# First block's attention with weights applied before the transposes and values computed feature-major

## The chip, the cores and the metric

The kernel runs on one core of one Trainium2 chip. The metric is the device time of one execution in microseconds (us), as the median of the runs shown. Engines are called by the profile's names: PE (matmuls, with PEld for the load of a stationary operand), DVE, ACT, POOL and SP.

## The reference, cut to what matters

Two transformer blocks run one after the other on 512 tokens of width 1024, all in float32. Only the attention of the first block is touched. For each of 8 heads (64 wide) and each block of 128 queries it computes three softmax attentions, and adds them with three gates per head and token:

```python
p_c = masked_softmax(s_c, cmp_end[None, :] <= t[:, None])   # compressed keys, 31 of them
o_c = einsum("bgrqk,bkgd->bqgrd", p_c, v_cmp)
p_s = masked_softmax(s_s, ...);  o_s = einsum(...)          # selected keys
p_w = masked_softmax(s_w, ...);  o_w = einsum(...)          # window
o = gb[..., 0:1] * o_c + gb[..., 1:2] * o_s + gb[..., 2:3] * o_w
...
mixed = concatenate([rmsnorm(y_conv, norm_conv_out), rmsnorm(y_att, norm_attn_out)], axis=-1)
h = h + rmsnorm(mixed @ w_out, norm_mix_post)
```

With 8 blocks of 64 keys and 16 selections every causal key is selected, so the selected and the window branch see the same causal keys and differ in their projections only.

## The kernel before, in words

Activations lie feature-major (128 features x 512 tokens) and weights stream in units of 128x2048, each split into a high and a low part, so that one product of 128x128 weights with 512 tokens is three matmuls (`products`, lines 417 to 419). Engines run side by side and meet at semaphores; each engine's own instructions run in the order written.

The attention is a software pipeline over turns `t` from -4 to 33, written out once for each engine (PE line 1016, ACT line 1238, DVE line 1484). Turns -4 to -1 hold the compressed branch, one block of 128 queries each (`c_scores`, `c_turn`, `c_values`, `c_combine`). Turns 0 to 31 start one job each. Job `j` is query block `j // 8`, head pair `j % 8 // 2` and branch `j % 2` (selected or window); its number of keys is 128, 256, 384 or 512 by block. A job goes through these steps:

- PE `scores(t)` (line 965): both heads' scores and the mask, into banks `2*(j%2)` and the next.
- DVE `maxima(t)` (line 1434): row maxima and their negatives. ACT `exps(t)` (line 1202): exponentials with row sums.
- PE `turn(t-1)` (line 981): transposes the probabilities, 2 x (1 to 4) pieces of 128x128, into bank 4 (and 5 from job 16 on). It waits for its exponentials, and for ACT to have copied the transposes of the job before out of bank 4.
- ACT `copy_turned(t-1)` (line 1213) and, from job 16, DVE `copy_turned` (line 1443): PSUM to SBUF.
- PE `values(t-2)` (line 995): probabilities stationary, 64 value columns moving, so the result lies tokens-major.
- DVE `combine(t-2)` (line 1450): reciprocal of the sum, times the gate, then for each head a multiply-add of 128x64 into `o_all`.

In a turn PE does scores, then chunks of input projections as filler (3 chunks of 3 matmuls in turns -4 to 7, 2 in turns 8 to 19, none later), then the turn, then the values. ACT does the exponentials of `t` before the copy of the older job. DVE also carries the short convolution and its norm in turns 8 to 30, and the weight splits. The convolution's column sums are on PE in turn 23, after POOL has added squares (line 2577); POOL then computes an inverse root in 12 small steps (`inverse_root`, line 701), which PE spreads to rows in turn 26 (line 1041).

After the loop PE fills with `mixed_products` (first half of the output projection). The attention norm takes row sums of squares from ACT, a root, a reciprocal, four scalings by DVE, and 16 transposes by PE (`mixed_turn`, line 1045) that turn `o_all` feature-major. Then a loop over `k` from 4 to 7 (line 1066) does the second half.

The second block's attention (`layer_pe`, line 2000) already computes its values with the value columns stationary and the two heads in the two column halves of the array (line 2133), and scales its probabilities on POOL (line 2597).

Of the kernel before, what the change touches and what calls it, by code (L numbers as in the profile page):

```python
# [31 lines left out]
P = 128  # L32
T = 512
# [68 lines left out]
def build(nc, w, x, mem, pos, pack, tables, cmask, w2, wg, rope2, out):  # L102
    ctx = ExitStack()
    with ctx:
# [55 lines left out]
        e_c = place("e_c", [P, 2, 2 * P], F32, b)  # L160
        pt_c = place("pt_c", [P, 2, 2 * P], F32, b)
        kvc = place("kvc", [P, 2, T], F32, a)
        vtok = place("vtok", [P, QB, 2 * P], F32, a)
        cosT = place("cosT", [P, T], F32, a)
# [6 lines left out]
        perm = place("perm", [P, P], F32, a)  # L171
        wg_s = place("wg_s", [P, 8 * 24], F32, a)
# [14 lines left out]
        probT = place("probT", [P, 2, 2, T], F32, b)  # L187

# [506 lines left out]
        ao_sq, ao_std, ao_inv, ao_n, ao_t = (sem("attn_norm_" + n) for n in ("squares", "std", "inv", "scaled", "turned"))  # L695
# [19 lines left out]
        LAG_TURN, LAG_VALUES, LAG_BACK = 1, 2, 3  # L715

# [15 lines left out]
        CONV_SQ_AT = {11: (0,), 16: (1,), 19: (2,), 22: (3,)}  # L732
        AT_CONV_SUM, AT_CONV_INV, AT_CONV_ROWS = 23, 24, 27
# [41 lines left out]
        def wide(j):  # L775
            return j >= 16

# [24 lines left out]
        def mixer1_pe(pe):  # L802
# [141 lines left out]
            def c_turn(i):  # L944
                pe.wait_ge(j_exp, i + 1)
                if i >= 1:
                    pe.wait_ge(j_pta, i)
                for e in range(2):
                    c0 = (2 * (i % 2) + e) * P
                    mm = pe.transpose(bank[:, 4, c0:c0 + P], e_c[:, i % 2, e * P:(e + 1) * P], ident[:, :])  # L950
                mm.then_inc(j_t, 1)

            def c_values(i):
                pe.wait_ge(j_pta, i + 1)
                if i == 0:
                    pe.wait_ge(vblk_ready, 4)
                else:
                    pe.wait_ge(j_o, i)
                for e in range(2):
                    mm = pe.matmul(bank[:, 6, e * 4 * HD:(e + 1) * 4 * HD], pt_c[:, i % 2, e * P:(e + 1) * P],  # L960
                                   vblk[:, :], start=True, stop=True)
                mm.then_inc(j_pv, 1)
# [18 lines left out]
            def turn(j):  # L981
                i = j // 8
                pe.wait_ge(j_exp, QB + 2 * (j + 1))
# [5 lines left out]
                for e in range(2):  # L989
                    for k in range(i + 1):  # L990
                        b_, c0 = (4 + e, k * P) if wide(j) else (4, (2 * e + k) * P)
                        mm = pe.transpose(bank[:, b_, c0:c0 + P], prob[:, j % 2, e, k * P:(k + 1) * P], ident[:, :])  # L992
                mm.then_inc(j_t, 1)

            def values(j):
                i, m, br, g = job(j)
                pe.wait_ge(j_pta, QB + j + 1)
                if wide(j):
                    pe.wait_ge(j_ptd, turned_by_dve(j))
                pe.wait_ge(j_o, QB + 2 * j)  # L1000
                for e in range(2):
                    c0 = (j % 2) * 2 * HD + e * HD
                    for k in range(i + 1):
                        mm = pe.matmul(bank[:, 6, c0:c0 + HD], probT[:, j % 2, e, k * P:(k + 1) * P],  # L1004
                                       vtok[:, k, br * P + g * HD:br * P + (g + 1) * HD], start=(k == 0), stop=(k == i))
                mm.then_inc(j_pv, 1)
# [9 lines left out]
            for t in range(-QB, JOBS + LAG_VALUES):  # L1016
                if t < 0:
                    c_scores(t + QB)
                elif t < JOBS:
                    scores(t)  # L1020
                gated_chunks(GATED_AT.get(t, 0))
                if t == -QB:
                    compressed_values()
                if t == JOBS:
                    pe.wait_ge(mix_lo, 4)
                    pe.wait_ge(lo_ready, U_OUT + 1)
                if t >= JOBS:
                    mixed_products(0, (t - JOBS,), range(4))
                if -QB <= t - LAG_TURN < 0:
                    c_turn(t - LAG_TURN + QB)  # L1030
                elif 0 <= t - LAG_TURN < JOBS:
                    turn(t - LAG_TURN)
                if -QB <= t - LAG_VALUES < 0:
                    c_values(t - LAG_VALUES + QB)
                elif t - LAG_VALUES >= 0:
                    values(t - LAG_VALUES)
# [8 lines left out]
            def mixed_turn(m):  # L1045
                if m == 0:
                    pe.wait_ge(ao_n, QB)
                if m >= 2:
                    pe.wait_ge(mix_lo, 4 + m - 1)
                for b_ in range(QB):  # L1050
                    mm = pe.transpose(bank[:, 6 + m % 2, b_ * P:(b_ + 1) * P], o_all[:, b_, m * P:(m + 1) * P], ident[:, :])
                mm.then_inc(ao_t, 1)

            pe.wait_ge(j_exp, QB + 2 * JOBS)
            pe.wait_ge(lo_ready, U_OUT + 2)
            mixed_products(1, (0, 1), range(4))
# [21 lines left out]
        def mixer1_act(act):  # L1078
# [112 lines left out]
            def c_e(i):  # L1191
                act.wait_ge(c_sub, i + 1)
                act.activation(e_c[:, i % 2, :], e_c[:, i % 2, :], ACT.Exp).then_inc(j_exp, 1)

            def c_copy(i):
                act.wait_ge(j_t, i + 1)
                if i >= 2:
                    act.wait_ge(j_pv, i - 1)
                c0 = 2 * (i % 2) * P
                act.activation(pt_c[:, i % 2, :], bank[:, 4, c0:c0 + 2 * P], ACT.Copy).then_inc(j_pta, 1)  # L1200

            def exps(j):
                n = (j // 8 + 1) * P
                act.wait_ge(j_neg, QB + j + 1)
                if j >= 2:
                    act.wait_ge(j_t, QB + j - 1)
                if j >= 4:
                    act.wait_ge(j_rec, j - 3)
                for e in range(2):
                    act.activation(prob[:, j % 2, e, 0:n], bank[:, 2 * (j % 2) + e, 0:n], ACT.Exp,  # L1210
                                   bias=jsm(j, 2, e), accum_out=jsm(j, 4, e)).then_inc(j_exp, 1)

            def copy_turned(j):
                n = (j // 8 + 1) * P
                act.wait_ge(j_t, QB + j + 1)
                if j >= 2:
                    act.wait_ge(j_pv, QB + j - 1)
                if wide(j):
                    act.activation(probT[:, j % 2, 0, 0:n], bank[:, 4, 0:n], ACT.Copy).then_inc(j_pta, 1)
                else:  # L1220
                    act.activation(probT[:, j % 2, :, 0:n], bank[:, 4, :].rearrange("p (e c) -> p e c", e=2)[:, :, 0:n],
                                   ACT.Copy).then_inc(j_pta, 1)

            def squares_of_block(b_):

                act.wait_ge(j_o, QB + 2 * 8 * (b_ + 1))
                if b_ >= 2:
                    act.wait_ge(ao_sq, b_ - 1)
                act.activation(ctmp[:, b_ % 2, :], o_all[:, b_, :], ACT.Square, accum_out=small[:, 32 + b_:33 + b_]).then_inc(ao_sq, 1)
# [8 lines left out]
            for t in range(-QB, JOBS + LAG_TURN):  # L1238
# [6 lines left out]
                if -QB <= t - LAG_TURN < 0:  # L1245
                    c_copy(t - LAG_TURN + QB)
                elif t - LAG_TURN >= 0:
                    copy_turned(t - LAG_TURN)
# [19 lines left out]
            act.wait_ge(ao_sq, QB)  # L1268
            act.activation(small[:, 36:40], small[:, 32:36], ACT.Sqrt, bias=eps_c[:, 0:1], scale=1.0 / 512).then_inc(ao_std, 1)
            for k in range(MEM_EARLY):  # L1270
                memory_hi(k)
            for m in range(4):
                act.wait_ge(ao_t, m + 1)
                act.activation(x_hi[:, 4 + m, :], bank[:, 6 + m % 2, :], ACT.Copy, scale=col("attn_out", m)).then_inc(mix_hi, 1)
# [11 lines left out]
        def mixer1_dve(dve):  # L1286
# [114 lines left out]
            def c_softmax(i):  # L1401
# [3 lines left out]
                if i >= 2:  # L1405
# [1358 lines left out]
```

## Time and profile before

| | |
|---|---|
| median of 3 runs | 2245.42 us (2244.32 to 2248.05) |
| profiled execution, own time | 2247.24 us |
| its span, first to last instruction | 2245.0 us |
| mean granted TensorE clock | 0.997 of 2.4 GHz |
| busy: PE, PEld, DVE, ACT, POOL | 2220.2, 1815.0, 1280.5, 845.4, 248.0 us |
| PE share of the chain that ended last | 87% |

A timeline row is: start in us, length in us, engine, line, operation, tiles, shapes, count, and in brackets the idle time before it with what ended it. The length of a PE row includes the array's latency, so the time that a group takes is read from its start to the start of what follows. A float32 matmul shows as two records, each with its load. A windows row is: stretch, length, then busy us and instruction count for PE, PEld, DVE, ACT, POOL, then the granted clock, the DMA share and GB/s.

### The profile page before, as it was taken

The page shows a single profiled execution, that of the slowest core. Times are in us where ns is not written, and L with a number is a line of the kernel's source. Part 1 is how long each engine was busy: PE and PEld are TensorE (multiplying, and loading weights), DVE is VectorE, ACT ScalarE, POOL GpSimd, SP SyncE. Part 2 cuts the span into 40 slices and gives each one's busy share as a digit, 9 for nine tenths or more (in the row PEclk, how much of TensorE's full clock was granted, in tenths as well). Part 3 has the DMA queues.
Part 4 walks back from the last instruction along what each step waited for, and adds up shares of the span by engine and source line. Part 5 has one row for each costly group of instructions (what it writes and reads, how often), then busy time and mean ns, then how long its engine had stood idle before and what let it go on. Part 6 is the DMA issues. An engine that isn't in the chain of part 4 may idle for free.

```text
span 2245.0 us, 29099 instructions
## 1 busy us (share of the span) xinstructions
PE 2220.2 (99%) x11292; PEld 1815.0 (81%) x11292; DVE 1280.5 (57%) x1948; ACT 845.4 (38%) x1299; POOL 248.0 (11%) x273
## 2 busy tenths in 40 slices
PE   9999999999999999999999999999999999999999
PEld 7877888898888888886678888888887668888887
DVE  6467656445444225999874444333889884544422
ACT  5545454354333225233544333222322543433321
POOL 3000032011000001013231000001003232000000
PEclk9999999999999999999999999999999999999999
DMA  6221033112222231321122222223321112322222
GB/s 222 101 76 57 20 118 129 55 70 100 101 105 93 94 113 71 113 75 57 56 77 85 103 93 94 103 102 108 107 81 57 39 69 82 113 101 104 94 100 87
DMA packets 30484, 203.44 MB, mean 91 GB/s; under 512 B 3504, under 2 KB 4144, under 8 KB 6704
## 3 DMA queue, kind: packets, MB, share of 16 engines
q1 hardware_dynamic: 29088, 197.34, 24.7%
q10 hardware_dynamic: 1296, 4.72, 0.6%
q8 instruction: 68, 1.11, 0.2%
q14 instruction: 32, 0.26, 0.0%
HBM read 199.95 MB, written 2.10 MB: 90 GB/s over the span
## 4 chain that ended last, share of the span: by engine, by line
PE 87%; DVE 8%; issue 2%; POOL 1%; ACT 1%; DMA 0%; ACTq 0%; DVEq 0%; POOLq 0%
PE bank L417 25%; PE bank L419 25%; PE bank L418 25%; DVE cy L2333 3%; PE bank L2133 1%; PE bank L2112 1%; PE bank L1004 1%; PE bank L2120 1%; DVE w_lo L303 1%; PE bank L975 1%; POOL acc L326 1%; PE bank L2012 1%; PE bank L992 1%; PE bank L1595 1%; PE bank L1572 1%
## 5 line engine op out<-in xcount | busy, mean ns | idle before, releaser
L417 PE MATMUL bank<-x_hi,w_hi 128*128 128x512 f32 (+1 forms) x2032 | 790.3, 389 | 5.7 <-DVE x_lo L1768 2.3
L419 PE MATMUL bank<-x_hi,w_lo 128*128 128x512 f32 (+1 forms) x2032 | 775.0, 381 | 0.0
L418 PE MATMUL bank<-x_lo,w_hi 128*128 128x512 f32 (+1 forms) x2032 | 774.2, 381 | 0.0
L303 DVE TENSOR_TENSOR w_lo<-w_raw,w_hi 128x2048 fp32r<-128x2048 f32 x167 | 386.2, 2312 | 412.6 <-ACT w_hi L299 412.6
L299 ACT ACTIVATE w_hi<-w_raw 128x2048 fp32r<-128x2048 f32 x167 | 319.7, 1916 | 585.9 <-PE bank L419 584.0
L417 PEld LDWEIGHTS bank<-x_hi,w_hi 128*128 128x128 f32 x2032 | 382.3, 188 | 83.4 <-issue 6.5
L419 PEld LDWEIGHTS bank<-x_hi,w_lo 128*128 128x128 f32 x2032 | 382.1, 188 | 74.8
L418 PEld LDWEIGHTS bank<-x_lo,w_hi 128*128 128x128 f32 x2032 | 382.6, 188 | 72.5 <-issue 2.9
L417 PE MATMUL bank<-f_hi,w_hi 128*128 128x512 f32 (+1 forms) x572 | 213.3, 373 | 0.0
L418 PE MATMUL bank<-f_lo,w_hi 128*128 128x512 f32 (+1 forms) x572 | 213.2, 373 | 0.0
L419 PE MATMUL bank<-f_hi,w_lo 128*128 128x512 f32 (+1 forms) x572 | 213.2, 373 | 0.0
L2333 DVE SCALAR_TENSOR_TENSOR cy<-la,gains,cy 128x512 f32<-128x512 f32 x240 | 172.8, 788 | 0.0
L565 DVE TENSOR_TENSOR bank<-bank,rbc 128x512 f32<-128x512 f32 x66 | 46.0, 697 | 167.7 <-PE bank L419 159.7
L418 PEld LDWEIGHTS bank<-f_lo,w_hi 128*128 128x128 f32 x572 | 107.7, 188 | 18.9
L417 PEld LDWEIGHTS bank<-f_hi,w_hi 128*128 128x128 f32 x572 | 107.7, 188 | 18.9
L419 PEld LDWEIGHTS bank<-f_hi,w_lo 128*128 128x128 f32 x572 | 107.7, 188 | 18.8
L326 POOL TENSOR_TENSOR acc<-acc,sq 128x512 f32<-128x512 f32 (+1 forms) x48 | 77.6, 1617 | 144.2 <-ACT sq L310 140.5
L2259 ACT ACTIVATE lprob<-lprob,small 128x129 f32<-128x129 f32 x128 | 50.5, 396 | 102.9 <-DVE small L2413 102.9
L554 ACT ACTIVATE f_hi<-bank 128x512 f32 x66 | 39.5, 598 | 115.5 <-DVE bank L571 115.5
L573 DVE TENSOR_TENSOR f_lo<-bank,f_hi 128x512 f32 x66 | 45.7, 692 | 58.4 <-ACT f_hi L554 58.4
L326 POOL TENSOR_TENSOR acc<-sq 128x512 f32<-128x512 f32 (+1 forms) x8 | 14.4, 1802 | 444.3 <-ACT sq L310 444.3
L552 ACT ACTIVATE silu<-bank 128x512 f32<-128x512 f32 x66 | 38.8, 588 | 54.7 <-DVE bank L565 54.5
(356 smaller groups left out, 2627.4 us busy)
## 6 DMA issues: line engine op xcount, KB each, us to landing
w_raw<-w_d SPq DMA_DIRECT2D x184, 1024.0 KB, 4.8
out_d<-h SPq DMA_DIRECT2D x8, 256.0 KB, 6.4
h<-x_d ACTq DMA_DIRECT2D x3, 512.0 KB, 9.3
tab<-rope_d ACTq DMA_DIRECT2D x2, 768.0 KB, 4.3
memT<-mem_d ACTq DMA_DIRECT2D x1, 1024.0 KB, 4.9
w_raw<-w_d SPq DMA_DIRECT2D x2, 256.0 KB, 3.9
h<-x_d ACTq DMA_DIRECT2D x2, 256.0 KB, 5.7
w_raw<-w_d SPq DMA_DIRECT2D x1, 512.0 KB, 6.6
```

The source lines that it names most:

```text
L299: act.activation(w_hi[:, u.slot, :], w_raw[:, u.slot, :], ACT.Copy).then_inc(hi_ready, 1)
L303: dve.tensor_tensor(w_lo[:, u.slot, :], w_raw[:, u.slot, :], w_hi[:, u.slot, :], ALU.subtract).then_inc(lo_ready, 1)
L326: pool.tensor_tensor(acc[:, 0:width], sq[:, 0, 0:width] if k == 1 else acc[:, 0:width], sq[:, k % 2, 0:width], ALU.add).then_inc(acc_ready, 1)
L417: pe.matmul(dst, wh[:, k, cols], hi[:, kx_, at:at + width], start=start, stop=False)
L418: pe.matmul(dst, wh[:, k, cols], lo[:, kx_, at:at + width], start=False, stop=False)
L419: return pe.matmul(dst, wl[:, k, cols], hi[:, kx_, at:at + width], start=False, stop=stop)
L552: act.activation(silu[:, :], g, ACT.Silu).then_inc(silu_done, 1)
L554: act.activation(pick(f_hi, j, i), up, ACT.Copy).then_inc(f_hi_done, 1)
L565: dve.tensor_tensor(g, g, rbc[:, :], ALU.mult).then_inc(gu_scaled, 1)
L573: dve.tensor_tensor(pick(f_lo, j, i), up, pick(f_hi, j, i), ALU.subtract).then_inc(f_lo_done, 1)
L2259: act.activation(row, row, ACT.Exp, bias=asm(j, 0, e), scale=-1.0, accum_out=asm(j, 4, e)).then_inc(A["exp"], 1)
L2333: dve.scalar_tensor_tensor(out=cy[:, m, :], in0=src, scalar=wt, in1=cy[:, m, :], op0=ALU.mult, op1=ALU.add).then_inc(l_tap, 1)
```

## The change

1. The weight of a branch (gate over row sum) is multiplied into the probabilities by POOL before the transposes, one instruction per job (and per compressed block), the last operand broadcast. DVE's `combine` becomes `weights` (reciprocal and gate only), done one turn after the scores.
2. The transposes and the copies come three turns after the scores (`LAG_J = 3`) instead of one. Probabilities and their transposes get a third buffer. In a turn PE does scores, turn, filler chunks, values.
3. The values of the three branches of a head pair are one accumulation group: value columns stationary (64 wide), transposed probabilities moving (128 columns), head 0 into partitions 0 to 63 and head 1 into 64 to 127 of one bank. 16 such groups, at odd turns, replace 32 `values` and 4 `c_values`; one DVE copy of 128x128 puts each into `o_all`, now feature-major.
4. The attention norm squares on ACT, adds four tiles on DVE (`add_squares`), takes column sums on PE, and spreads the inverse root back over rows; DVE multiplies four tiles by it. The 16 transposes go.
5. On POOL the three convolution adds and the inverse root now stand between the scalings, at turns 17, 20, 23 and 25.

```diff
+        LAG_J, PAIRS = 3, QB * 4
+        CONV_ADD_AT = {17: 1, 20: 2, 23: 3}
+        def value_pair(t):
+            if t == JOBS + 2:
+                return PAIRS - 1
+            return (t - 5) // 2 if t % 2 and 5 <= t < JOBS + 2 else None
...
             def turn(j):
                 i = j // 8
-                pe.wait_ge(j_exp, QB + 2 * (j + 1))
+                pe.wait_ge(j_scaled, QB + j + 1)
                 pe.wait_ge(j_pta, QB + j)
...
+            def values(q):
+                i, m, _, g = job(2 * q)
+                pe.wait_ge(j_pta, QB + 2 * q + 2)
...
+                dst = [bank[HD * e:HD * e + HD, 6, 0:P] for e in range(2)]
                 for e in range(2):
+                    pe.matmul(dst[e], vblk[:, m * HD:(m + 1) * HD], pt_c[:, i, e * P:(e + 1) * P], start=True, stop=False)
+                for br in range(2):
                     for k in range(i + 1):
+                        v = vtok[:, k, br * P + g * HD:br * P + (g + 1) * HD]
+                        for e in range(2):
+                            mm = pe.matmul(dst[e], v, turned_of(2 * q + br)[:, e, k * P:(k + 1) * P],
+                                           start=False, stop=(br == 1 and k == i))
...
-            for t in range(-QB, JOBS + LAG_VALUES):
+            for t in range(-QB, JOBS + LAG_J):
...
+                if -QB <= t - LAG_J < 0:
+                    c_turn(t - LAG_J + QB)
+                elif t - LAG_J >= 0:
+                    turn(t - LAG_J)
                 gated_chunks(GATED_AT.get(t, 0))
...
+                    mixed_products((t - JOBS) // 2, ((t - JOBS) % 2,), range(4))
+                if value_pair(t) is not None:
+                    values(value_pair(t))
...
+            mixed_products(1, (1,), range(4))
             pe.wait_ge(lo_ready, U_OUT + 3)
+            pe.wait_ge(ao_sum, QB)
+            column_sums(pe, bank[:, 7, 0:QB], o_sq[:, :]).then_inc(ao_step, 1)
             mixed_products(2, (0,), range(4))
+            pe.wait_ge(ao_step, AO_INV)
+            pe.wait_ge(j_o, PAIRS)
+            spread(pe, bank[:, 6, :], small[:, 36:40]).then_inc(ao_step, 1)
             mixed_products(2, (1,), range(4))
...
# ACT
-                if -QB <= t - LAG_TURN < 0:
-                    c_copy(t - LAG_TURN + QB)
-                elif t - LAG_TURN >= 0:
-                    copy_turned(t - LAG_TURN)
+                if -QB <= t - LAG_J < 0:
+                    c_copy(t - LAG_J + QB)
+                elif t - LAG_J >= 0:
+                    copy_turned(t - LAG_J)
...
# DVE
+                if -QB <= t - 1 < 0:
+                    c_weights(t - 1 + QB)
+                elif 0 <= t - 1 < JOBS:
+                    weights(t - 1)
+                if 0 <= t - LAG_J < JOBS and wide(t - LAG_J):
+                    copy_turned(t - LAG_J)
+                if value_pair(t - 1) is not None:
+                    values_out(value_pair(t - 1))
+X
+            for t in range(-QB, JOBS + 1):
...
+                elif t - 1 >= 0:
+                    n = ((t - 1) // 8 + 1) * P
+                    p = prob_of(t - 1)[:, :, 0:n]
+                    pool.wait_ge(j_w, t)
+                    pool.tensor_tensor(p, p, jsm(t - 1, 8).unsqueeze(2).to_broadcast([P, 2, n]), ALU.mult).then_inc(j_scaled, 1)
+                if t in CONV_ADD_AT:
...
+                if t == AT_CONV_INV + 1:
+                    inverse_root(pool)
```

## Rows read from the trace of the kernel before

**Rows 1.** The page, busy time of each engine

```profile
PE 2220.2 (99%) x11292; PEld 1815.0 (81%) x11292; DVE 1280.5 (57%) x1948; ACT 845.4 (38%) x1299; POOL 248.0 (11%) x273
```

**Rows 2.** Windows, turns 24 to 31

```profile
220.00:252.00 32.00, 30.49 (x231) 23.53 (x229) 27.35 (x67) 19.18 (x49) 3.68 (x13) 1.00 0.16 61
```

**Rows 3.** Timeline of PE: first rows of turns 20, 24, 32, and of the last loop

```profile
207.90 0.59 PE L975 MATMUL bank<-kTx,qT 64*128 64x384 f32 x1
...
223.19 0.69 PE L975 MATMUL bank<-kT,qT 64*128 64x512 f32 x1
...
255.26 0.48 PE L417 MATMUL bank<-x_hi,w_hi 128*128 128x512 f32 x1
...
277.93 0.47 PE L417 MATMUL bank<-x_hi,w_hi 128*128 128x512 f32 x1
```

**Rows 4.** Timeline of PE, turn 29: turn, values, next scores

```profile
244.56 1.06 PE L992 MATMUL bank<-ident,prob 128*128 128x128 f32 x8
245.46 1.90 PE L1004 MATMUL bank<-vtok,probT 128*128 128x64 f32 x16
247.29 0.69 PE L975 MATMUL bank<-kTx,qT 64*128 64x512 f32 x1
```

**Rows 5.** The chain that ended last: one compressed block's values

```profile
129.60 0.87 PE bank L960 x4
```

**Rows 6.** Timeline of PE in the second block: values in column halves, their neighbours

```profile
1060.34 0.39 PE L418 MATMUL bank<-x_lo,w_hi 128*128 128x512 f32 x1
1060.57 0.40 PE L419 MATMUL bank<-x_hi,w_lo 128*128 128x512 f32 x1
1060.89 0.66 PE L2133 MATMUL bank<-lband,lv 128*64 128x128 f32 x8
...
1099.77 0.39 PE L2133 MATMUL bank<-lband,lv 128*64 128x128 f32 x4
1100.09 0.48 PE L2112 MATMUL bank<-lq 64*128 64x256 f32 x1
```

**Rows 7.** Timelines of DVE (turns 24, 25, 28) and ACT (copy of turn 28)

```profile
224.57 1.22 DVE L1439 TENSOR_REDUCE jcol<-bank 128x2 f32<-128x1024 f32 x1 [0.76 <-PE bank L978]
...
228.77 1.23 DVE L1439 TENSOR_REDUCE jcol<-bank 128x2 f32<-128x1024 f32 x1
...
241.07 1.22 DVE L1439 TENSOR_REDUCE jcol<-bank 128x2 f32<-128x1024 f32 x1
...
243.87 0.59 ACT L1219 ACTIVATE probT<-bank 128x512 f32<-128x512 f32 x1
```

**Rows 8.** Timelines of DVE and ACT, turn 21

```profile
212.84 0.95 DVE L1439 TENSOR_REDUCE jcol<-bank 128x2 f32<-128x768 f32 x1
...
215.16 0.49 ACT L1219 ACTIVATE probT<-bank 128x384 f32<-128x384 f32 x1
```

**Rows 9.** Lines by form, POOL: busy us, mean ns, then idle before

```profile
L326 POOL TENSOR_TENSOR acc<-acc,sq 128x512 f32<-128x512 f32 x42 | 73.2, 1743 | 135.4 <-ACT sq L310 132.3
L2597 POOL TENSOR_TENSOR lprob<-lprob,small 128x256 f32<-128x256 f32 x64 | 39.1, 612 | 155.4 <-DVE small L2401 155.4
...
L2569 POOL TENSOR_TENSOR acc<-rbc 128x512 f32<-128x512 f32 x1 | 1.0, 1040 | 6.2 <-ACT rbc L399 6.2
```

**Rows 10.** Timeline of POOL: first and last of the 12 root steps

```profile
228.94 0.20 POOL L706 TENSOR_TENSOR jcol<-jcol 128x4 f32<-128x4 f32 x1 [6.79 <-DVE jcol L1481]
...
232.05 0.20 POOL L713 TENSOR_TENSOR rcol_c<-jcol 128x4 f32<-128x4 f32 x1
```

**Rows 11.** Timeline of DVE, turn 30: low halves of the convolution

```profile
251.88 1.41 DVE L1514 SCALAR_TENSOR_TENSOR x_lo<-cv,gains,x_hi 128x512 fp32r<-128x512 f32 x2
```

**Rows 12.** Timeline of PE, second block: column sums behind a wait

```profile
1063.28 1.05 PE L335 MATMUL bank<-ones,la 128*128 128x1 f32 x8 [1.73 <-POOL la L2611]
```

**Rows 13.** Windows around those column sums

```profile
1062.00:1064.00 2.00, 0.72 (x7) 0.72 (x7) 1.92 (x9) 0.30 (x1) 1.97 (x3) 1.00 0.17 70
...
1066.00:1068.00 2.00, 2.00 (x12) 1.03 (x10) 1.92 (x8) 0.58 (x2) 0.74 (x2) 0.51 0.00 0
```

More of the change, by code:

```diff
@@ L159, in build @@
         b = [a[0]]
[L160 to L161 removed]
+        e_c = place("e_c", [P, QB, 2 * P], F32, b)
         kvc = place("kvc", [P, 2, T], F32, a)
         vtok = place("vtok", [P, QB, 2 * P], F32, a)
+        cos_at = a[0]
         cosT = place("cosT", [P, T], F32, a)
@@ L171, in build @@
         perm = place("perm", [P, P], F32, a)
+        b = [a[0]]
+        pt_c = place("pt_c", [P, QB, 2 * P], F32, b)
+        o_sq = place("o_sq", [P, T], F32, b)
         wg_s = place("wg_s", [P, 8 * 24], F32, a)
@@ L694, in build @@
             "turned_copied_dve", "pv", "out"))
-        ao_sq, ao_std, ao_inv, ao_n, ao_t = (sem("attn_norm_" + n) for n in ("squares", "std", "inv", "scaled", "turned"))
+        ao_sq, ao_sum, ao_step, ao_n = (sem("attn_norm_" + n) for n in ("squares", "added", "step", "scaled"))
+        AO_SUMS, AO_STD, AO_INV, AO_ROWS = 1, 2, 3, 4
+        j_scaled = sem("job_scaled")
         JOBS = QB * 8
@@ L949, in c_turn @@
                     c0 = (2 * (i % 2) + e) * P
-                    mm = pe.transpose(bank[:, 4, c0:c0 + P], e_c[:, i % 2, e * P:(e + 1) * P], ident[:, :])
+                    mm = pe.transpose(bank[:, 4, c0:c0 + P], e_c[:, i, e * P:(e + 1) * P], ident[:, :])
                 mm.then_inc(j_t, 1)
[L953 to L962, printed above, removed]
             def scores(j):
@@ L1235, in memory_hi @@
                 square(act, NORM_MEM, k, memT[:, k, :], MEM)
-            for t in range(-QB, JOBS + LAG_TURN):
+            for t in range(-QB, JOBS + LAG_J):
                 if t < 0:
@@ L1455, in combine, with values_out, add_squares @@
                 dve.tensor_tensor(jsm(j, 8), jsm(j, 6), gate[:, i, 6 * m + 1 + br:6 * m + 5 + br:3], ALU.mult).then_inc(j_w, 1)
[L1456 to L1466 removed]
+            def values_out(q):
+                i, m, _, g = job(2 * q)
+                dve.wait_ge(j_pv, q + 1)
+                dve.tensor_copy(o_all[:, m, i * P:(i + 1) * P], bank[:, 6, 0:P]).then_inc(j_o, 1)
+            def add_squares(b_):
+                dve.wait_ge(ao_sq, b_ + 1)
+                dve.tensor_reduce(o_sq[:, b_ * P:(b_ + 1) * P], ctmp[:, b_ % 2, :].rearrange("p (m t) -> p t m", m=4),
+                                  AX, ALU.add).then_inc(ao_sum, 1)
             def memory_lo(k):
@@ L1483, in mixer1_dve @@
             dve.wait_ge(gate_ready, QB)
-            for t in range(-QB, JOBS + LAG_VALUES):
+            for t in range(-QB, JOBS + LAG_J + 1):
                 if t < 0:
```

178 lines of the change are left out of this document (69 added, 109 removed).

## The prediction

> **What bounds the kernel now.** I read the page first: PE is busy 99% of the span and no other engine over 57% (DVE) [rows 1], so only what lengthens or shortens PE's own sequence counts. Then the windows of the attention: in turns 24 to 31 PE still shows 30.5 of 32.0 us, but DVE has 27.4 [rows 2], so relief for PE is soon met by DVE or by waits. Then PE's timeline, for the time of each stage. Turns 20 to 23 take 15.3 us, turns 24 to 31 take 32.1, and from there to the last loop over k it is 22.7 [rows 3]. Last, the timelines of DVE and ACT beside PE, for the chain that a turn hangs on. All sums are against the profiled execution (2247.24 us, span 2245.0); the median of the runs is 2245.42, and I put the same difference on it.
>
> **Prices on PE.** Old values: 16 records from 245.46 to 247.29, 0.115 us each [rows 4]. A transpose is 0.11 (8 in 0.90) [rows 4], a compressed block's values 0.87 [rows 5]. The new form stands in the trace already: the second block's values are also 128 rows by 64 columns with 128 moving columns, heads in column halves. There 8 records take 0.66, of which the last 0.27 is latency, so 0.056 each; the group starts 0.32 after its neighbour where neighbours are 0.23 apart, and 4 records take 0.32 to the next scores [rows 6]. So a group costs 0.056 per record and about 0.1 at each end. A head pair has 12, 20, 28 or 36 records in query blocks 0 to 3: 0.87, 1.32, 1.77, 2.2 us, against 0.92, 1.84, 2.76, 3.66 for the two old jobs. The end pieces are where a rule speaks against the change. The Trainium skill (TensorEngine Tiling (Array Packing), Tiling Modes, Key Properties) says that a change of tiling mode drains the array. The rows agree that there is a price, 0.1 at each end; if a full latency of 0.27 went at both ends of 16 groups, the sum would be some 5 us worse.
>
> **Before turn 20.** PE has filler chunks there and sets the pace. Removed: 4 compressed blocks at 0.87 = 3.5; values of jobs 0 to 17, 8x4 + 8x8 + 2x12 = 120 records = 13.8; transposes of jobs 17 and 18, now later, 12 x 0.11 = 1.3. Added: pairs 0 to 7, 4 x 0.87 + 4 x 1.32 = 8.8. Net 9.8 less. Against it: a turn now stands ahead of the chunks that used to cover its wait, and it still waits for ACT's copy of the job before, which is queued behind the newest exponentials. I take 0.4 for several short waits net of one that goes (between 0 and 2). **9.4 gained.**
>
> **Turns 20 to 31, the step that I think decides.** Without chunks, PE's turn(t-3) waits for copy(t-4), which ACT issues in turn t-1 behind exps(t-1). The longer lag does not loosen this: the chain still runs from the newest scores. For 512 keys: first score to the reduction 1.38 (223.19 to 224.57), reduction to ACT's copy 2.80 (241.07 to 243.87), copy to the turn 0.69 [rows 3, 4, 7], turn to values 0.90 [rows 4], together 5.77. At odd t the values of a whole pair follow, 2.2, and only then the next scores: at least 8.0 us for two jobs. Before, the same chain with one job's 1.83 was 7.6 for two, hidden by PE's own work of some 3.9 per job (a turn is 4.0 [rows 3], of it 0.90 and 1.83 [rows 4], the rest scores, about 1.2). So block 3 is as slow as before although PE works only 2 x 1.2 + 2 x 0.9 + 2.2 = 6.4 us in those 8. For 384 keys: 1.15 (the 1.38 less the shorter scores) + 2.32 + 0.49 + 0.10 [rows 8] + 0.66 + 1.77 = 6.5.
>
> Two new waits lie on top, both of PE for POOL. The scaling: 0.612 for 256 elements, and 1.04 for 512 where one operand is read twice; 1.74 where two are [rows 9]. I take 2.1 for 1024 and 1.6 for 768, as its second operand is a column; the ends are 0.6 (no growth with size) and 3.5.
> - Turn 23: the column sums of the convolution wait for POOL's third add, now behind scaled(22), which waits for DVE's weights of turn 23. From the scores of turn 22: 1.15; DVE's turn 22 2.8 (reduction 0.95 [rows 8], and by estimate 0.5 for small ones, 0.5 and 0.2 for copies, 0.65 for the squares); reduction and weights of turn 23 1.5; scaling 1.6; add 1.3 (1.04 to 1.74 [rows 9]); sums 1.0 [rows 12]: 9.4. With 6.5 for turns 20 and 21: 15.9 against 15.3, **0.6 lost**.
> - Turn 26: PE's spread waits for the inverse root, now behind scaled(24). From the scores of turn 24: 1.38; DVE's turn 24 4.0 (4.20 before [rows 7] less 0.4 for two multiply-adds plus 0.2 for the copy); reduction and weights of turn 25 1.7; scaling 2.1; root 3.3 [rows 10]; spread 0.5: turn 27 starts at 13.0. Scores 1.2, turn 0.9 and a pair of 1.77 bring turn 28 to 16.9, and two rounds of 8.0 turn 32 to 32.9, against 32.1: **0.8 lost**.
>
> **After turn 31.** PE has 1.8 more (two transposed jobs later), 4.4 for two pairs instead of 3.66 for two jobs (0.75), 1.5 for column sums and spread instead of 16 transposes at 0.11 (0.3 less), and some 0.3 for restarts. DVE's turn 30 carries two low halves (1.41 [rows 11]), add_squares (about 0.65, half of a 1024-element reduction [rows 7]) and a copy, so exps(31) and the turn behind it come some 1.4 late. The norm's chain (copy, squares, add; then root and reciprocal) is covered by blocks of 12 products, 12 x 0.23 = 2.7 [rows 6]; the first scaled tile, behind three memory tiles on DVE, is not quite: 0.5. **4.5 lost.** What POOL, ACT and DVE do of the memory norm keeps its place behind this. No transfer moves; SP's queue and the four DMAs of ACT are untouched.
>
> **The clock.** In the second block a wait of 1.73 for POOL followed by one-column sums [rows 12] was followed by a granted clock of 0.51, the lower of its two levels (1.2 GHz), after 1.00 [rows 13]. The change makes two such places, turn 23 (a wait of 1.6, then sums) and turn 26 (3 us idle). At the lower level the next scores (1.2) take twice as long, and behind the spread some 0.6 more: 1.0 or 1.9. I take one of the two, 1.4 (ends 0 and 2.9). The Trainium skill (TensorE: Matmul & The Clock Gate, Part 1) says that the slow level is the default and activity lifts it; the rows agree.
>
> **Sum:** -9.4 + 0.6 + 0.8 + 4.5 + 1.4 = -2.1: 2245.4 - 2.1 = **2243.3**.
>
> **Rivals.**
> - *PE's work decides everywhere.* Removed in all: 3.5 + 320 records x 0.115 = 36.8 + 1.8; added 384 records x 0.056 = 21.5, 16 x 0.2 = 3.2, sums and spread 1.5: 15.9 less, 2229.5. For it: 99% busy. Against it: turn 29 of the trace starts 0.69 after the start of the 0.59 us copy, not when PE is free [rows 4, 7]. 0.10.
> - *The clock holds.* Without the 1.4: 2241.9. For it: the pauses have other lengths than the one seen. 0.22.
> - *POOL is dear.* 3.5 for 1024 elements and 2.6 for 768, as in the dearest row: 1.4 later at turn 26, 1.0 at turn 23: 2245.7. For it: DVE's convolution and POOL read the same memory at once. Against it: 0.612 in the second block, beside a busy DVE. 0.11.
> - *Slower: the low clock stays.* From turn 24 on PE works 6.4 of 8.0 us a pair; at 0.51 [rows 13] it needs 12.5, 4.5 more than the chain, and small matmuls follow that may not lift the clock. From 1.5 pairs on (-2.1 + 6.7) the kernel is past no change by more than can be told; for two pairs it is -2.1 + 9.0: 2252.3. Against it: before, all of turns 24 to 31 ran at 1.00 [rows 2]. 0.12.
> - *My forecast*, 0.45, with 2239 to 2247.5 as its own range (the ends of the waits and of the clock above).
>
> **How the numbers follow.** A measurement of this kernel can tell about 0.2%, 4.5 us, from no change: 2240.9 and 2249.9. Faster: the first rival whole, four tenths of the second, a sixth of the forecast: 0.26. Slower: most of the last rival and a little of the forecast: 0.14. The rest, 0.60, is within. Range: 2236.5 to 2250.0, which leaves out the first rival and most of the slower one.
>
> **What would show it.** Right: PE rows of the 128x64 form at 0.056; turn 20 about 9 us earlier than before; pairs of turns from 28 on 8.0 us apart, with PE idle before the transposes, released by ACT's copy; a wait for POOL before the column sums of turn 23 and before the spread of turn 26; the last loop at most 4 us earlier. Wrong: transposes that start as soon as PE is free; turns 24 to 31 in under 29 us (PE's work decides) or over 36 (the clock); scalings over 3 us.

## The result, and the profile after

The changed kernel takes 2250.38 us (median of ten runs), the kernel before 2245.59 us in the same series: the ratio is 1.0018, 95% interval 1.001 to 1.0026, which is 2.2 to 5.8 us. By the medians it is 4.8 us slower where 2.1 us faster was forecast, and 0.4 us above the range. One of the ten runs of the kernel before took 7339 us; without it their median is 2245.42 us. The profiled execution took 2251.5 us with a span of 2249.7 us (2247.24 and 2245.0 before).

The page of the changed kernel, busy time of each engine, shows what was meant to happen: against [rows 1] PE works 9 us less, and POOL 44 us more.

```profile
PE 2211.1 (98%) x11336; PEld 1794.9 (80%) x11336; DVE 1282.0 (57%) x1900; ACT 844.9 (38%) x1295; POOL 291.9 (13%) x309
```

So PE lost its work and the kernel still got longer: PE waits. Its timeline shows where (first rows of turns 20, 24, 27, 28 and 30, the waits that decide, the last loop over k; they answer to [rows 3, 4]). In the second and third row PE waits in turns 22 and 23:

```profile
200.37 0.59 PE L984 MATMUL bank<-kTx,qT 64*128 64x384 f32 x1
...
209.28 0.85 PE L1001 MATMUL bank<-ident,prob 128*128 128x128 f32 x6 [1.25 <-ACT probT L1221]
...
213.44 1.52 PE L1001 MATMUL bank<-ident,prob 128*128 128x128 f32 x6 [2.24 <-ACT probT L1221]
...
218.70 1.05 PE L339 MATMUL bank<-ones,z 128*128 128x1 f32 x8 [1.20 <-POOL z L2591]
219.68 0.83 PE L984 MATMUL bank<-kT,qT 64*128 64x512 f32 x1
...
233.42 0.82 PE L346 MATMUL bank<-ident,rcol_c 128*128 128x128 f32 x4 [2.74 <-POOL rcol_c L719]
234.17 1.22 PE L984 MATMUL bank<-kT,qT 64*128 64x512 f32 x1
...
237.74 0.44 PE L1016 MATMUL bank<-pt_c,vblk 128*64 128x128 f32 x4
...
239.41 0.69 PE L984 MATMUL bank<-kTx,qT 64*128 64x512 f32 x1
...
244.29 1.07 PE L1001 MATMUL bank<-ident,prob 128*128 128x128 f32 x8 [1.37 <-ACT probT L1221]
245.29 0.44 PE L1016 MATMUL bank<-pt_c,vblk 128*64 128x128 f32 x4
245.56 1.92 PE L1021 MATMUL bank<-probT,vtok 128*64 128x128 f32 x32
247.40 0.69 PE L984 MATMUL bank<-kTx,qT 64*128 64x512 f32 x1
...
282.54 0.39 PE L421 MATMUL bank<-x_hi,w_hi 128*128 128x512 f32 x1
```

Turn 20 starts 7.5 us earlier than before (200.37 for 207.90). Turns 20 to 23 then take 19.3 us for 15.3. Turns 24 to 31 take 36.0 for 32.1: their last values start at 254.81 and end some 0.9 later, at 255.7. From there to the last loop it is 26.8 for 22.7. In sum the loop starts 4.6 us late, and the whole span is 4.7 us longer: in these two profiles the loss lies ahead of the loop.

The timelines of DVE and POOL in turns 20 to 23 show what stretched them. The convolution steps (L1373, L1375) and the low half (L815) are longer here than the same operations before, and each ends after the POOL row in which it started. The two row reductions (L1434, L1459) are no longer than elsewhere:

```profile
203.04 1.47 POOL L2585 TENSOR_TENSOR prob<-prob,jcol 128x768 f32<-128x768 f32 x1 [1.97 <-DVE jcol L1450]
203.55 1.24 DVE L1373 TENSOR_SCALAR cv<-z,gains 128x512 f32<-128x512 f32 x1
204.47 1.45 POOL L2591 TENSOR_TENSOR z<-z 128x512 f32<-128x512 f32 x1
204.83 1.64 DVE L1375 SCALAR_TENSOR_TENSOR cv<-z,gains,cv 128x511 f32<-128x511 f32 x1
...
207.88 1.47 POOL L2585 TENSOR_TENSOR prob<-prob,jcol 128x768 f32<-128x768 f32 x1 [1.96 <-DVE jcol L1450]
208.19 1.70 DVE L1375 SCALAR_TENSOR_TENSOR cv<-z,gains,cv 128x510 f32<-128x510 f32 x1
...
210.53 0.95 DVE L1434 TENSOR_REDUCE jcol<-bank 128x2 f32<-128x768 f32 x1
...
212.03 1.47 POOL L2585 TENSOR_TENSOR prob<-prob,jcol 128x768 f32<-128x768 f32 x1 [2.69 <-DVE jcol L1450]
212.54 1.03 DVE L1459 TENSOR_REDUCE o_sq<-ctmp 128x128 f32<-128x512 f32 x1
...
214.98 1.47 POOL L2585 TENSOR_TENSOR prob<-prob,jcol 128x768 f32<-128x768 f32 x1 [1.48 <-DVE jcol L1450]
215.46 2.06 DVE L815 TENSOR_TENSOR w_lo<-w_raw,w_hi 128x1024 fp32r<-128x1024 f32 x1
216.41 2.24 POOL L2591 TENSOR_TENSOR z<-z 128x512 f32<-128x512 f32 x1
```

The same three steps of the convolution in the kernel before (timeline of DVE, turns 20 and 21):

```profile
211.66 0.48 DVE L1370 TENSOR_SCALAR cv<-z,gains 128x512 f32<-128x512 f32 x1
212.18 0.75 DVE L1372 SCALAR_TENSOR_TENSOR cv<-z,gains,cv 128x511 f32<-128x511 f32 x1
...
215.16 0.74 DVE L1372 SCALAR_TENSOR_TENSOR cv<-z,gains,cv 128x510 f32<-128x510 f32 x1
```

It is a wait, not a slower rate. POOL's scaling at 207.88 ends at 209.35, and DVE's step beside it ends 0.54 later (alone 0.74); the scaling at 214.98 ends at 216.45, DVE's low half 1.07 later (alone 1.22, at 222.60 in the kernel before). It goes both ways: DVE's low half ends at 217.52, and POOL's third add, beside it from 216.41, ends 1.13 after that, where the same add in the kernel before takes 1.26 to 1.28. So the later instruction does nearly all of its work after the earlier one has ended, whatever its length: what is left is 0.13 to 0.20 us less than its time alone. Not every DVE instruction waits. Those that read PSUM are not touched: a copy of 128x384 at 214.99, beside the scaling, takes 0.56 as before, and the reduction over 1024 elements at 228.97, beside a scaling that lasts from 228.22 to 230.11, takes 1.23 as in [rows 7]. A row reduction out of SBUF is not touched either: the one at 212.54 takes 1.03 beside POOL, and 1.02 to 1.07 in run e7 below with POOL idle. The Trainium skill (SBUF — State Buffer, Who interferes with whom) says that DVE instructions with two SBUF inputs, or in a mode that uses two ports, share a port pair with GpSimd (POOL), that it is held for a whole instruction, and that the later one fully blocks. The rows above agree.

The granted clock (windows of 1 us; the third number from the end) was at its lower level, 0.50, in three stretches, at about 213 to 216.7, 220 to 223.5 and 233.7 to 237.2 us. A window out of each:

```profile
215.00:216.00 1.00, 1.00 (x10) 1.00 (x12) 1.00 (x2) 0.96 (x3) 1.00 (x1) 0.50 1.00 426
...
222.00:223.00 1.00, 1.00 (x7) 0.67 (x5) 0.97 (x1) 0.00 (x0) 0.00 (x0) 0.50 0.00 0
...
235.00:236.00 1.00, 1.00 (x4) 0.00 (x0) 0.00 (x0) 0.00 (x0) 0.21 (x1) 0.50 0.00 0
```

Each followed a stretch in which PE had waited: 2.24 before the first, 1.20 and one-column sums before the second, 2.74 before the third.

### The profile page after: what moved, and what is told of

The parts are those of the page before. It is cut to its first block, busy times and chain, and to the rows that moved or that the text cites. A ratio compares the mean times of both kernels' runs of the same rounds, so it can differ in the third digit from the quotient of the medians.

```text
span 2249.7 us, 29110 instructions
## 1 busy us (share of the span) xinstructions
PE 2211.1 (98%) x11336; PEld 1794.9 (80%) x11336; DVE 1282.0 (57%) x1900; ACT 844.9 (38%) x1295; POOL 291.9 (13%) x309
## 3 DMA queue, kind: packets, MB, share of 16 engines
q8 instruction: 69, 1.13, 0.2%
## 4 chain that ended last, share of the span: by engine, by line
PE 78%; DVE 7%; issue 1%; POOL 1%; ACT 1%; DVEq 0%; POOLq 0%; ACTq 0%
PE bank L421 24%; PE bank L423 23%; PE bank L422 23%; DVE cy L2335 3%; PE bank L2135 1%; PE bank L2114 1%; PE bank L2122 1%; DVE w_lo L307 1%; POOL acc L330 1%; PE bank L2014 1%; PE bank L1597 1%; PE bank L1574 1%; DVE bank L2348 1%; DVE bank L2367 0%; PE bank L339 0%
## 5 line engine op out<-in xcount | busy, mean ns | idle before, releaser
L422 PEld LDWEIGHTS bank<-f_lo,w_hi 128*128 128x128 f32 x572 | 107.7, 188 | 18.9
L2612 POOL TENSOR_TENSOR lprob<-lprob,small 128x256 f32<-128x256 f32 x64 | 39.1, 612 | 157.0 <-DVE small L2403 156.9
```

Source lines behind the costliest of these rows:

```text
L422: pe.matmul(dst, wh[:, k, cols], lo[:, kx_, at:at + width], start=False, stop=False)
L2612: pool.tensor_tensor(row, row, asm(j, 12).unsqueeze(2).to_broadcast([P, 2, P]), ALU.mult).then_inc(A["scaled"], 1)
```

## The experiments

Theories: **A**, the blocking of DVE and POOL, whose lateness goes on through exponentials and copies to the turns; **B**, the low clock after PE's pauses; **C**, the turn that waits for ACT's copy of the job before, behind the newest exponentials; **D**, added later, the mere length of the scaling on the path. Each row of the table gives the median beside that of the kernel before in the same series, the ratio with its interval, and from the profile the start of turn 20, of turn 24, and of the memory norm's column sums, which stand behind all that was changed.

| kernel | us, before | ratio (95%) | turn 20 | turn 24 | sums |
|---|---|---|---|---|---|
| before | | | 207.90 | 223.19 | 286.22 |
| changed | 2250.38, 2245.59 | 1.0018 (1.001 to 1.0026) | 200.37 | 219.68 | 290.70 |
| e1 two columns | 2238.68, 2245.62 | 0.997 (0.9958 to 0.9983) | 198.51 | 213.67 | 279.39 |
| e2 copy first | 2246.36, 2245.62 | 1.0004 (0.9995 to 1.0013) | 197.65 | 217.51 | 288.66 |
| e3 clock filler | 2248.15, 2245.62 | 1.0004 (0.9995 to 1.0013) | 199.49 | 218.82 | 287.60 |
| e4 diagonal | 2254.1, 2245.62 | 1.0037 (1.0024 to 1.0051) | 205.50 | 222.53 | 296.27 |
| e5 weights first | 2245.62, 2246.63 | 0.9993 (0.9984 to 1.0002) | 200.19 | 215.83 | 284.97 |
| e6 weights and copy first | 2241.34, 2246.63 | 0.9975 (0.9965 to 0.9985) | 196.81 | 213.94 | 281.27 |
| e7 scaled by ACT | 2232.5, 2246.63 | 0.994 (0.9927 to 0.9953) | 196.68 | 210.51 | 272.60 |
| e8 before, spare scaling | 2256.49, 2246.63 | 1.0048 (1.0035 to 1.0061) | 207.72 | 229.13 | 295.38 |
| e9 ACT scaling alone | 2238.94, 2245.24 | 0.9972 (0.996 to 0.9983) | 199.34 | 213.74 | 279.19 |

Gains "against the changed kernel" below are differences of the two distances to the kernel before; the changed kernel stands at +4.8. The intervals put such a difference at about 3 us either way, so a second measure helps: in the profiles, the time from the first row of turn -4 (118.87 us in the changed kernel), ahead of which nothing was changed, to the sums. By it e1 is 10.7 us shorter than the changed kernel, e2 2.2, e3 2.3, e5 5.8, e6 8.8, e7 17.3 and e9 10.5; e4 is 5.3 longer; e8 is 9.3 longer than the kernel before.

**e1, POOL's volume out, its waits kept.**

```diff
-                    p = prob_of(t - 1)[:, :, 0:n]
+                    p = prob_of(t - 1)[:, :, 0:2]
-... jsm(t - 1, 8).unsqueeze(2).to_broadcast([P, 2, n]) ...
+... jsm(t - 1, 8).unsqueeze(2).to_broadcast([P, 2, 2]) ...
```

> POOL scales two key columns of each head instead of all keys; every wait, order and instruction count stays, so the weights of the branches are left out of all other columns. Theory A (DVE's work runs slower beside POOL's scalings, and the late reductions hold up the turns): DVE's convolution steps go back from 1.24, 1.64 and 1.70 us to 0.48, 0.75 and 0.75, POOL's third add from 2.24 to about 1.3, turns 20 to 23 from 19.3 to about 15.5 us, turn 20 starts 1 to 2 us earlier, and the kernel ends 5 to 7 us earlier: about 2244. Theory B (the low clock after PE's pauses is the loss): the pauses for POOL's add and for the inverse root stay, so does the low clock; no more than 1 to 2 us earlier. Theory C (the turn waits for ACT's copy of the job before, which stands behind the newest exponentials): the copy keeps its place; PE's waits for the copy stay as long as they are, 1.2 to 2.2 us, and the kernel ends no more than 2 us earlier.

Measured: 6.9 us under the kernel before, 11.7 against the changed one; more than A asked for, and far from B and C. Turns 20 to 23 take 15.2 us, and POOL's third add 1.27. The timelines of DVE and POOL in turns 20 to 22 have both cases in one kernel:

```profile
201.34 1.26 POOL L2591 TENSOR_TENSOR z<-z 128x512 f32<-128x512 f32 x1
201.50 0.28 DVE L1455 COPY o_all<-bank 128x128 f32<-128x128 f32 x1
201.70 1.19 DVE L1373 TENSOR_SCALAR cv<-z,gains 128x512 f32<-128x512 f32 x1
202.92 0.75 DVE L1375 SCALAR_TENSOR_TENSOR cv<-z,gains,cv 128x511 f32<-128x511 f32 x1
...
205.09 0.20 POOL L2585 TENSOR_TENSOR prob<-prob,jcol 128x4 f32<-128x4 f32 x1 [2.48 <-DVE jcol L1450]
205.40 0.74 DVE L1375 SCALAR_TENSOR_TENSOR cv<-z,gains,cv 128x510 f32<-128x510 f32 x1
```

Beside POOL's add, which stayed, the first step still takes 1.19; the copy out of PSUM beside the same add keeps its 0.28; the steps with no POOL beside them are back at 0.75 and 0.74. The waits for ACT's copy did not go (8.2 us in all), so C is no rival but a second part.

**e2, ACT copies first.** In ACT's loop, `copy_turned(t - LAG_J)` and `c_copy` move ahead of `exps(t)` and `c_e`.

> ACT does the copy of job t-3 ahead of the exponentials of job t. Theory C: PE's waits for ACT's copy (1.2, 1.3, 2.2, 1.4, 1.8 and 1.6 us in turns 21, 22, 23, 29, 31 and 32) go; pairs of turns from 28 on come down from 8.0 us towards PE's work of 6.4 or DVE's of about 7; the kernel ends 4 to 6 us earlier, about 2245. Theory A: DVE is late whatever ACT's order; the waits move to the scores or to the scaling, and no more than 2 us are won. Theory B: only what the clock gains by shorter pauses, 0 to 3 us.

Measured: 4.1 us against the changed kernel by the medians, as C said, but 2.2 by the profiles, about the most that A allowed: the time does not part them. The list of PE's waits shows the next one in line:

```profile
PE bank L1001 <- DVE probT L1443: 7.2, 5, 2.2
PE bank L346 <- POOL rcol_c L719: 3.8, 1, 3.8
```

The waits for ACT's copy became waits for DVE's copy of the other half, late behind the blocked convolution, and for POOL. In the profile the gain lies ahead of turn 20 (2.7 us) and from turn 28 on, where a pair takes 6.9 us; between turns 20 and 28 1.7 us of it are lost again.

**e3, PE kept busy in its waits.**

```diff
+            def run_on(count):
+                pe.wait_ge(fill_out, 12)
+                for _ in range(count):
+                    pe.matmul(bank[:, 7, P:2 * P], ident_b[:, :], mask_b[:, 0:P], start=True, stop=True)
```

> PE runs small matmuls whose result nobody reads while it waits: 10, 15 and 30 of them ahead of the transposes of turns 21, 22 and 23, 18 ahead of the convolution's column sums and 50 ahead of the spread. Nothing else is changed. Theory B: the granted clock stays at 1.00 from 212 to 238 us, the scores of turns 24 and 27 take 1.2 us instead of 2.2, and the kernel ends 3 to 5 us earlier, about 2246. Theories A and C: the low clock is a follower; where it fell in a wait nothing is won, and what it added to the scores of turns 24 and 27 and to the work behind them, 1.6 us each, is the most that comes back: 2247 to 2249.

Measured: 2.3 us against the changed kernel by the medians and by the profiles, inside what A and C allowed (2247 to 2249) and short of B's 3 to 5; with this noise the time alone settles little. The timeline of PE says more. With the filler the granted clock stays at 1.00 through turn 23, where it had fallen in the changed kernel, and turns 20 to 23 take 19.3 us all the same. With the filler up to the spread, the scores of turn 27 run at full clock (0.69 each); those of turn 25, behind the column sums of turn 23, do not (1.22), although 18 small matmuls ran ahead of the wait for POOL's add:

```profile
217.84 1.05 PE L339 MATMUL bank<-ones,z 128*128 128x1 f32 x8 [1.64 <-POOL z L2601]
...
221.30 1.22 PE L985 MATMUL bank<-kT,qT 64*128 64x512 f32 x1
...
228.99 2.96 PE L994 MATMUL bank<-mask_b,ident_b 128*128 128x128 bf16 x50
231.89 0.65 PE L346 MATMUL bank<-ident,rcol_c 128*128 128x128 f32 x4
232.47 0.69 PE L985 MATMUL bank<-kT,qT 64*128 64x512 f32 x1
```

The stretch from 220 to 223.5 us is at 0.50 as in the changed kernel. From turn 24 to turn 28 this profile is 2.2 us shorter (17.5 for 19.7), 1.4 of it in the scores and transposes of turn 27 (2.2 for 3.6). So the low clock is a real cost behind the spread, and none in turn 23, where PE waits for POOL's add next.

**e4, the weight in the transposes.**

```diff
-                        mm = pe.transpose(bank[:, b_, c0:c0 + P], prob_of(j)[:, e, k * P:(k + 1) * P], ident[:, :])
+                        mm = pe.matmul(bank[:, b_, c0:c0 + P], prob_of(j)[:, e, k * P:(k + 1) * P], diag[:, j % 2, e, :], start=True, stop=True)
...
+                for e in range(2):
+                    act.activation(diag[:, j % 2, e, :], ident[:, :], ACT.Copy, scale=jsm(j, 8, e)).then_inc(j_scaled, 1)
```

> The weight goes into the transposes: ACT writes a diagonal matrix of the 128 weights of each head (two activations of 128x128 per job), and PE multiplies the probabilities by it instead of by the identity. POOL has no scaling of jobs left, and its adds and the inverse root are free to go early; ACT copies job t-3 ahead of the exponentials of t. Theories A and C together: DVE's convolution steps take 0.48 and 0.75 us, the root stands behind no scaling, turns 20 to 23 take about 14 us and turns 24 to 31 about 28; the kernel ends 8 to 14 us earlier than the changed one, 2236 to 2242, and so 3 to 9 us ahead of the kernel before. If a product with the diagonal takes longer than a transpose (0.11 us), 224 of them cost 1 us for each 0.005 us. Theory B alone: the gain is what the clock gives back, 3 to 5 us.

Measured: slower than all but e8. PE's timeline, turn 28, has the reason: eight products with a diagonal are 16 records and take 1.93 us up to the next scores, where eight transposes took 0.97 (248.59 to 249.56 in the changed kernel).

```profile
241.06 2.00 PE L1002 MATMUL bank<-e_c,prob 128*128 128x128 f32 x16
242.99 0.69 PE L985 MATMUL bank<-kTx,qT 64*128 64x512 f32 x1
```

The jobs have 160 transposes (not the 224 of my expectation), so this costs 160 x 0.12 = 19 us. The kernel is only 3.7 slower than the changed one: some 15 us must have been gained elsewhere, as A and C would have it, and were more than paid for on PE.

**e5 and e6, the same work in another order.** On DVE:

```diff
+                if 0 <= t - 1 < JOBS:
+                    weights(t - 1)
                 if t < 0:
                     c_softmax(t + QB)
                 elif t < JOBS:
                     maxima(t)
...
-                elif 0 <= t - 1 < JOBS:
-                    weights(t - 1)
```

> Only DVE's order is changed: the weights of job t-1 stand ahead of the maxima of job t instead of behind them, so that POOL's scaling (0.73 to 1.89 us) runs beside DVE's reduction and copies out of PSUM, which the scalings were not seen to slow, and is over when DVE's work on SBUF (convolution, low halves) begins. All work stays. Theory A (that work waits for POOL's scaling, or POOL for it): the convolution steps come back to 0.48 and 0.75 us, POOL's third add to about 1.3, and most of what run e1_two_columns won (11.7 us) comes back with every weight applied: 2239 to 2244. Against it, the maxima may have to wait for the exponentials of the job before, up to 0.6 us in some turns, and the small negation behind them may now wait for POOL. Theory D (it is the length of the scaling on the path from exponentials to transposes that e1 took away, not the contention): nothing comes back, 2248 to 2251.

Measured: 5.8 us against the changed kernel, half of e1's and short of A's 2239 to 2244, with every weight applied. The three convolution steps are back at 0.47, 0.75 and 0.73, POOL's third add at 1.27, and turns 20 to 23 take 15.6 us, with each scaling as long as before (1.47 and 1.90): D's "nothing" is out. The new order also lets a scaling start sooner behind its exponentials, and what that gives by itself was not measured apart. Part of what is missing stands where it was suspected. The timelines of POOL and DVE in turn 28:

```profile
228.38 1.90 POOL L2585 TENSOR_TENSOR prob<-prob,jcol 128x1024 f32<-128x1024 f32 x1
228.43 1.22 DVE L1434 TENSOR_REDUCE jcol<-bank 128x2 f32<-128x1024 f32 x1
229.69 0.61 DVE L1436 TENSOR_SCALAR jcol<-jcol 128x2 f32<-128x2 f32 x1
```

The reduction out of PSUM keeps its 1.22, and the negation of two columns, 0.17 alone, ends at 230.30, just after POOL's 230.28. The exponentials wait for it.

> The order of e5_weights_first on DVE and that of e2_copy_first on ACT (copy of job t-3 ahead of the exponentials of t) together. In e2 the waits for ACT's copy were taken over by waits for DVE's copy, which came late behind convolution steps slowed to 1.64 and 1.70 us. If A holds, those steps are short here, and the waits for either copy go: pairs of turns from 28 on in 6.6 to 7.4 us instead of 8.0, the kernel 3 to 5 us under e5_weights_first: 2235 to 2240, and so ahead of the kernel before by 5 to 10. If the gains are the same one counted twice: no better than the better of e2 (2246.4) and e5.

e6 adds e2's order on ACT. Measured: 10.1 us against the changed kernel, 4.3 more than e5, as e2 alone had 4.1: within the noise the two gains add up. Turns 28 and 29 take 7.3 us (230.05 to 237.37). The waits for either copy did not go, as was expected: those for ACT's did, but PE still waits 7.5 us for DVE's copy (five times, up to 2.2 us).

**e7 and e9, the scaling of blocks 2 and 3 on ACT.**

```diff
+            def scaled(j):
+                act.wait_ge(j_w, j + 1)
+                for e in range(2):
+                    p = prob_of(j)[:, e, 0:(j // 8 + 1) * P]
+                    act.activation(p, p, ACT.Copy, scale=jsm(j, 8, e)).then_inc(a_scaled, 1)
...
+                if ACT_FROM <= t - 2 < JOBS:
+                    scaled(t - 2)
```

with `ACT_FROM = 16`; POOL keeps jobs 0 to 15. e7 also has e2's order, e9 has not.

> From job 16 on ACT scales the probabilities instead of POOL (two activations of 128x384 or 128x512 per job, ahead of the copy of job t-3 and the exponentials of t); POOL scales jobs 0 to 15 only. All work stays. Theory A: without POOL beside it DVE's steps in turns 17 to 30 are as short as in the kernel before, the inverse root stands behind no scaling: 2236 to 2242. ACT's turn in block 3 is then 1.9 us of exponentials and copy plus 1.1, under PE's 3.2; where it also makes high halves (1.33 us, turns 28 and 29) it is late by about 1 us each. Theory D: the path from exponentials to transposes still has a scaling in it, about as long as POOL's: 2246 or more.

> Run e7_scaled_by_act without its change of order on ACT: ACT scales jobs 16 to 31, but the copy of job t-3 stands behind the exponentials of t again. This parts e7's gain (17.9 us from the changed kernel, each against the kernel before) into scaling off POOL and order of the copy. Theory A (POOL beside DVE is the main loss): most of it is the scaling, 2234 to 2239; the rest, 2 to 5 us, is the order, about what e2 (4.7 us) and the step from e5 to e6 (4.3) gave. If the order were the main part: 2243 or more, with PE waiting 1.2 to 2.2 us for ACT's copy in most turns from 21 on.

Measured: e9 is 6.3 us under the kernel before, about what e1 gave with the weights left out (6.9): taken off POOL, the scaling costs nothing that these runs can tell. (The expectation of e9 misstates two gains: e7's against the changed kernel is 18.9 and e2's 4.1.) e7 is 14.1 under the kernel before, better than forecast, since the order is worth 7.8 here and not 2 to 5: with DVE on time, a copy that comes early is used. In e7 DVE's three convolution steps are back at 0.48, 0.75 and 0.74. PE's waits are almost gone (list of PE's waits, 116 to 300 us, e7):

```profile
PE bank L1005 <- DVE probT L1455: 2.1, 4, 1.1
PE bank L1005 <- ACT probT L1231: 1.7, 1, 1.7
...
PE bank L339 <- POOL z L2603: 0.7, 1, 0.7
```

**e8, the cost alone, in the kernel before.**

```diff
+                    p = spare[:, :, 0:n]
+                    v = vtok[:, :, :].rearrange("p (e b) c -> p e (b c)", e=2)[:, :, 0:n]
+                    pool.wait_ge(j_w, t)
...
+                    pool.tensor_tensor(p, v, gains[:, 0:2].unsqueeze(2).to_broadcast([P, 2, n]), ALU.mult).then_inc(spare_done, 1)
```

> The kernel before, with one added piece of work that nobody waits for: POOL writes a spare buffer, once per job and as large as the job's probabilities (256 to 1024 elements), as soon as the job's weight is there. The convolution's adds and the inverse root stand between these as in the changed kernel. Theory A: DVE's convolution steps (0.48, 0.75 us) and low halves (1.22 for 128x1024) run to 1.2 to 2.1 us, DVE's 27.4 us in turns 24 to 31 become some 30, and the kernel ends 3 to 8 us later than before: 2249 to 2253. Theory D: work that no one waits for costs at most what the root is late, 0 to 2 us.

Measured: 9.9 us slower than before, above A's 3 to 8. No one waits for the added work, so this loss is not the length of a scaling on the path. The timelines of POOL and DVE, turn 22:

```profile
215.91 1.47 POOL L2583 TENSOR_TENSOR spare<-vtok,gains 128x768 f32<-128x768 f32 x1 [2.95 <-DVE jcol L1457]
...
216.26 1.67 DVE L1374 SCALAR_TENSOR_TENSOR cv<-z,gains,cv 128x510 f32<-128x510 f32 x1
217.34 1.71 POOL L2589 TENSOR_TENSOR z<-z 128x512 f32<-128x512 f32 x1
217.96 1.64 DVE L1377 TENSOR_TENSOR cv<-cv,bg 128x512 f32<-128x512 f32 x1
```

Not all of it is DVE's: the convolution's adds stood behind the spare work and PE waited 1.2 for the last one, and from 221 to 232 us the granted clock was 0.58 in the mean, after waits of 1.1 and 2.4 us for ACT's copies. At that clock the column sums of turn 23 and the scores of turn 24 took 1.8 and 2.2 us instead of 1.0 and 1.2. How the 9.9 us divide was not measured.

## Why the prediction was wrong

**Where the miss lies.** The sum was -2.1 us and the medians say +4.8. In the profiles the terms missed by 1.9 us before turn 20, 3.4 in turns 20 to 23, 1.7 in turns 24 to 31 with the clock, and -0.4 after turn 31.

**The step that failed** is "Turns 20 to 31", in the durations that it took from the kernel before for work that now has POOL beside it: the time that DVE and POOL wait for each other's instructions stood in it at nothing. For turn 23 it put DVE's turn 22 at "2.8" behind a reduction 1.15 after the scores, and POOL's add at "1.3". Measured from the scores of turn 22 (206.90): the reduction came 3.6 after them (210.53), since the three convolution steps of turns 20 to 22 had taken 2.6 us more than alone (1.24, 1.64 and 1.70 for 0.48, 0.75 and 0.74); the add took 2.24. Those two are 2.5 + 0.9 = 3.4 us, and all of the miss of this stage: 19.3 for 15.9 us. The other links held: DVE's turn 2.96, reduction and weights 1.5, scaling 1.47 for 1.6, sums 0.98 for 1.0. With POOL's volume out (e1) the stage takes 15.2.

The sign stood in the trace of the kernel before, beside POOL's third add (timelines of POOL and DVE, turn 23): a product of two columns, 0.16 elsewhere, takes 1.18 and ends 0.02 after POOL's add.

```profile
220.89 1.26 POOL L2577 TENSOR_TENSOR z<-z 128x512 f32<-128x512 f32 x1 [10.84 <-ACT z L1256]
220.99 1.18 DVE L1455 TENSOR_TENSOR jcol<-jcol,gate 128x2 f32<-128x2 f32 x1
```

**Turns 24 to 31**: 36.0 us for 32.9 plus the 1.4 of the clock. Nearly all of the 3.1 lies ahead of turn 28. DVE's low half in turn 24 took 2.04 for 1.22, beside a scaling, 0.8 more; the rest goes with the low clock: the reduction of turn 24 came 2.1 after its scores instead of 1.38, and the scores and transposes of turn 27 took 3.6 (234.17 to 237.74) where 2.1 was put.

**The clock** was mis-sized: "one of the two" places and 1.4, and three stretches came. Those behind the column sums and the spread ran some 6.8 us of span at half speed, by estimate 3.4 lost at most, some of it where PE would have waited for POOL anyway; e3 got 2.2 back in turns 24 to 27. The one in turn 23 is covered by the wait for POOL's add that follows. The two waits that were foreseen were no longer than forecast (1.20 and 2.74 for 1.6 and 3); the third, 2.24 for ACT's copy behind the late exponentials, was not foreseen. The working had a slip, too: scores of 1.2 at half speed lose 1.2, not 1.0.

**Before turn 20**: 7.5 gained for 9.4, of which 0.5 is no effect of the change: turn -4, ahead of which nothing was changed, starts at 118.87 instead of 118.35 (117.88 to 119.13 in the variants). The new form was priced right (12 records in 0.81 for 0.87; the 36 of a last pair in 245.29 to 247.40, 2.1 for 2.2, and no sign of the dearer ends). e1 gives back 1.2 of turns 0 to 19, e2 2.9: the 0.4 for ACT's copy was too small.

**Right**: the chain behind ACT's copy (turns 28 and 29 took 7.99 us for 8.0, released by the copy), both waits of PE for POOL, the scaling's own price (1.89 and 1.47 for 2.1 and 1.6), and the stage after turn 31 (26.8 for 27.2). Of the rivals, "POOL is dear" had the place (DVE's convolution and POOL at the same memory) and the wrong victim: it charged POOL, and the longer part fell on DVE, whose lateness the chain carries on to PE.

What stays open: how much of the changed kernel's loss the clock would be by itself. e3 held it up in two of the three places, one of which costs nothing, and its runs spread from 2243.6 to 2249.3; its profile is of the fastest of them.

## What to carry to other kernels

When work is moved to POOL, look at what DVE does at that moment: give each DVE instruction of the kinds that were seen to wait (products, sums and scalings with all operands in SBUF, however small) the rest of POOL's instruction as extra time, and follow it to whoever waits for DVE. If ACT has the room, ACT takes such work for next to nothing (e9 against e1), and if not, put POOL's work beside DVE's reads of PSUM (e5). Look for a DVE instruction that ends with a POOL instruction in the trace you start from: here it was there. Then look for the engine order that made the wait, since freeing DVE and copying first were worth more together (18.9 us) than the two alone added up (11.1 and 4.1).

## What the runs showed of the hardware that I had not expected

- A DVE instruction of two columns waits out a POOL instruction of 1024 elements: 0.61 for 0.17 us (e5). Its size does not spare it, its kind can: a reciprocal of two columns at 256.90 in the changed kernel, beside a scaling, takes 0.17, and the product behind it 0.54, up to the end of that scaling.
- A float32 product with a 128x128 stationary operand takes twice a transpose of the same size (0.24 and 0.12 us, e4; two records against one), while the 128x64 form with the same 128 moving columns takes 0.115 for its two records (32 records in 1.84 us).
- In e3 the clock fell behind the column sums in the same stretch as without the filler (220 to 223.5 us), although PE had been kept busy up to a wait of 1.64 us.
